# Two fused blocks with PEER experts on one core: more tokens by fetched rows, thirty expert blocks in float32, part of the gates on ScalarE

## The reference

```python
def peer_ffn(h, w_query, sub_keys_1, sub_keys_2, expert_u, expert_v):
    ...
    best, pos = lax.top_k(cand, PEER_TOPK)                 # 16 of the candidates, for each of 8 heads
    idx = jnp.take_along_axis(cand_idx, pos, axis=-1)      # expert numbers
    g = jax.nn.softmax(best, axis=-1)
    u = expert_u[idx]
    act = jax.nn.gelu(jnp.einsum('td,thkd->thk', xc, u))
    w = g * act
    return jnp.einsum('thk,thkd->td', w, expert_v[idx])
```

## Time and profile before

| | |
|---|---|
| runs | 1281.8, 1286.84, 1285.42 us; median 1285.42 |
| profiled execution | 1281.33 us, its span 1280.0 us |
| TensorE busy | 1222.2 us, 95% of the span, 11350 matmuls |
| VectorE busy | 1037.5 us, 81% |
| ScalarE busy | 641.9 us, 50% |
| GpSimd busy | 308.0 us, 24% |
| mean granted clock of TensorE | 0.994 |
| moved by DMA | 266.41 MB, mean 208 GB/s |

### The profile page before, as it was taken

The page is one execution under the profiler, slowest core; times in us unless marked ns, Lnnn a source line. Parts: engine busy times, 40 slices in busy tenths (PEclk is TensorE's granted clock), DMA queues, the critical chain, the costliest instruction groups (busy, mean ns, idle before and its releaser), DMA issues.

```text
span 1280.0 us, 26647 instructions
## 1 busy us (share of the span) xinstructions
PE 1222.2 (95%) x11350; PEld 1033.1 (81%) x11350; DVE 1037.5 (81%) x1640; ACT 641.9 (50%) x859; POOL 308.0 (24%) x202
## 2 busy tenths in 40 slices
PE   6899888999999999999999999999999999999997
PEld 5545674888844546648998899999999999999996
DVE  5865884899956776777499999999998888989884
ACT  5663231767635435646245455554445554445553
POOL 0322221154500000000102600000003656555640
PEclk9999998999999999999999999999999999999999
DMA  7530003755566322357165675555558999999981
GB/s 308 189 118 12 2 2 132 284 210 197 204 225 250 108 101 97 134 196 251 47 235 199 238 263 204 198 198 198 198 191 302 343 344 359 364 340 388 342 318 34
DMA packets 51350, 266.41 MB, mean 208 GB/s; under 512 B 5136, under 2 KB 5408, under 8 KB 32544
## 3 DMA queue, kind: packets, MB, share of 16 engines
q1 hardware_dynamic: 40192, 226.76, 49.3%
q0 software_dynamic: 10160, 35.96, 7.4%
q10 hardware_dynamic: 880, 1.99, 0.5%
HBM read 262.04 MB, written 2.10 MB: 206 GB/s over the span
## 4 chain that ended last, share of the span: by engine, by line
PE 65%; DVE 21%; DMA 5%; issue 4%; ACT 4%; ACTq 0%; POOL 0%; DVEq 0%; POOLq 0%
PE bank L674 18%; PE bank L677 18%; PE bank L680 18%; DMA arena<-in_expert_rows,arena 5%; PE bank L1103 2%; DVE X L2263 2%; DVE HT L2263 2%; DVE ring L2263 2%; PE bank L1317 2%; DVE arena L2316 1%; PE bank L754 1%; PE bank L1281 1%; DVE ring L1780 1%; PE bank L821 1%; PE bank L1270 1%
## 5 line engine op out<-in xcount | busy, mean ns | idle before, releaser
L674 PE MATMUL bank<-arena 128*128 128x256 f16 (+3 forms) x720 | 216.3, 307 | 0.6 <-DVE arena L1450 0.4
L677 PE MATMUL bank<-arena 128*128 128x256 f16 (+3 forms) x720 | 216.2, 307 | 0.0
L680 PE MATMUL bank<-arena 128*128 128x256 f16 (+3 forms) x720 | 216.1, 307 | 0.0
L1450 DVE SCALAR_TENSOR_TENSOR arena<-ring,arena 128x2048 f16<-128x2048 f32 (+1 forms) x59 | 133.8, 2273 | 31.8 <-ACT arena L2492 31.7
L3186 POOL DMA_INDIRECT arena<-in_expert_rows,arena x32 | 74.2, 2318 | 285.0 <-DVE arena L2316 283.9
L2492 ACT ACTIVATE arena<-ring 128x2048 f16<-128x2048 f32 (+1 forms) x59 | 111.2, 1891 | 28.9 <-PE bank L680 28.9
L2929 ACT CAST arena<-arena 128x448 f16<-128x448 f32 x64 | 36.0, 565 | 136.1 <-PE bank L680 133.7
L3186 POOL DMA_INDIRECT arena<-in_expert_v,arena x32 | 85.9, 2685 | 62.9 <-DVE arena L2334 54.2
L2263 DVE SCALAR_TENSOR_TENSOR HT<-ring,HT 128x2048 f16<-128x2048 f32 x41 | 93.8, 2287 | 8.0 <-ACT HT L2898 7.9
L680 PEld LDWEIGHTS bank<-arena 128*128 128x128 f16 x720 | 70.5, 98 | 36.8 <-issue 0.6
L674 PEld LDWEIGHTS bank<-arena 128*128 128x128 f16 x720 | 70.5, 98 | 36.7 <-issue 2.0
(11 more groups left out here) (382 smaller groups left out, 3713.2 us busy)
## 6 DMA issues: line engine op xcount, KB each, us to landing
ring<-in_expert_u SPq DMA_DIRECT2D x64, 1024.0 KB
ring<-in_expert_v SPq DMA_DIRECT2D x64, 1024.0 KB
ring<-in_w_in_n SPq DMA_DIRECT2D x24, 1024.0 KB, 4.7
ring<-in_w_up_t SPq DMA_DIRECT2D x22, 1024.0 KB, 5.0
ring<-in_w_down_n SPq DMA_DIRECT2D x11, 1024.0 KB, 4.8
ring<-in_w_out_n SPq DMA_DIRECT2D x8, 1024.0 KB, 4.7
ring<-in_w_query_t SPq DMA_DIRECT2D x8, 1024.0 KB, 4.8
ring<-in_w_in_t SPq DMA_DIRECT2D x3, 1024.0 KB
```

Of the source, the lines that this page charges most:

```text
L674: pe.matmul(out_, stat[0], mov[0], start=start, stop=False, skip_group_check=shared)
L677: pe.matmul(out_, stat[0], mov[1], start=False, stop=False, skip_group_check=shared)
L680: return pe.matmul(out_, stat[1], mov[0], start=False, stop=stop, skip_group_check=shared)
L1450: nv.scalar_tensor_tensor(out=lo, in0=ld.slot(i), scalar=W_UP, in1=hi, op0=ALU.mult, op1=ALU.subtract).then_inc(s["split_lo"], 1)
```

## The change

NG becomes 56 tokens, in three groups of 32, 16 and 8 tokens: in a fetch of the second group a token has 8 partitions, in one of the third 16. There are 56 fetches from each matrix, so 112, into NFETCH = 4 buffers, of which one is free early and the others when the search has ended. NT becomes 200 and there are 25 groups of gates. 48 of the 56 row dots are moved into turns 28 to 63 of the u stage. Whole blocks are now 30: 0, 1, 2, every third up to 63, and 28, 34, 40, 46, 52, 58. Split blocks in u use two pairs of buffers; the third lies where float32 tokens are kept, which whole blocks need to the end. `rows_gained` moves the multiplication of `h_rows` by the gain from GpSimd to VectorE. The last one-hot operation moves from VectorE to ScalarE, `gated_hi`, eight activations per group, each with a scale per partition. The small DMAs that place rows grow from 4 to 28, those for places and gates from 8 to 56.

```diff
-NG = 32
+ROW_GROUPS = (32, 16, 8)
+NG = sum(ROW_GROUPS)
+NFETCH = 4
 NT = S - NG
-WHOLE = 3
+WHOLE = [q for q in range(64) if q < 3 or q % 3 == 0 or (q > 26 and q % 6 == 4)]
+SPLIT = [q for q in range(64) if q not in WHOLE]
...
-ROWS_IN = [max(0, min(NG, 5 * (n - 63) // 4)) for n in range(128)]
-ROWS_OUT = [max(0, min(NG, n - 90)) for n in range(128)]
-ROW_GELU = 90
+ROWS_IN = [max(0, min(NG, 4 * (n - 27) // 3 if n < 64 else n - 15)) for n in range(128)]
+ROWS_OUT = [max(0, min(NG, (15 * (n - 72)) // 14)) for n in range(128)]
+ROW_GELU = next(n for n in range(128) if ROWS_IN[n] == NG) + 1
...
             for hf in range(2):
-                pe.matmul(ps.tile("fin", 1, hf)[128 - NG:128, :], m.row_sel, m.row_sums[:, hf * 512:(hf + 1) * 512],
-                          start=True, stop=True)
+                for a, sel in enumerate(m.row_sel):
+                    pe.matmul(ps.tile("fin", 1, hf)[:, :], sel, m.row_sums[a][:, hf * 512:(hf + 1) * 512],
+                              start=(a == 0), stop=(a == len(m.row_sel) - 1))
...
-        c = step(nv.tensor_tensor(oh2[:, 1], oh2[:, 0], of[3], ALU.mult))
-        after(c)
-        nv.tensor_tensor(oh2[:, 0], oh2[:, 0], of[2], ALU.mult).then_inc(s["one_hots"], 1)
+        nv.tensor_tensor(oh2[:, 1], oh2[:, 0], of[3], ALU.mult).then_inc(s["one_hots_lo"], 1)
...
+    def rows_gained():
+        nv.wait_ge(s["rows_placed"], 16 * sum(128 // n for n in ROW_GROUPS))
+        nv.wait_ge(s["row_gain_landed"], 16)
+        for h_ in m.h_rows:
+            nv.tensor_tensor(h_, h_, m.row_gain, ALU.mult).then_inc(s["h_rows"], 1)
...
-        expert_lo(q + 2 - WHOLE)
+        if q >= 62 or q + 2 in SPLIT:
+            expert_lo(SPLIT.index(q + 2) if q < 62 else len(SPLIT) + q - 62)
...
+    def gated_hi(g):
+
+        t0, oh2 = NG + 8 * g, m.oh2[g % 2]
+        na.wait_ge(s["one_hots_lo"], g + 1)
+        for i in range(8):
+            one = oh2[:, 0, i // 2, :, i % 2]
+            ins = na.activation(one, one, ACT.Copy, scale=m.slot_scale[:, t0 + i:t0 + i + 1])
+        ins.then_inc(s["one_hots"], 1)
...
-        expert_hi(q + 3 - WHOLE)
+        if q >= 61 or q + 3 in SPLIT:
+            expert_hi(SPLIT.index(q + 3) if q < 61 else len(SPLIT) + q - 61)
+        if q + 2 in GATES_IN:
+            gated_hi(GATES_IN[q + 2])
         if q in GATES_IN:
             keep_gates(GATES_IN[q])
...
+    for n, first in zip(ROW_GROUPS, ROW_FIRST):
+        of, to = slice(first, first + n), slice(first, first + n)
+        for i in range(128 // n):
+            rows, at = slice(i * n, (i + 1) * n), slice(i * n, (i + 1) * n)
+            ng.dma_start(m.row_at[rows, to], m.places[of, at]).then_inc(s["rows_placed"], 16)
+            ng.dma_start(m.row_gate[rows, to], gate[of, at]).then_inc(s["rows_placed"], 16)
...
-    read += [ps.full("u", q) if q < WHOLE else (s["expert_lo"], q - WHOLE + 1) for q in range(64)]
+    read += [ps.full("u", q) if q in WHOLE else (s["expert_lo"], SPLIT.index(q) + 1) for q in range(64)]
```

More of the change, by code:

```diff
@@ L30 @@
 NSLOTS = 5
-NG = 32
+ROW_GROUPS = (32, 16, 8)
+NG = sum(ROW_GROUPS)
+ROW_FIRST = [sum(ROW_GROUPS[:a]) for a in range(len(ROW_GROUPS))]
+NFETCH = 4
 NT = S - NG
-NK = 128 // NG
 GROUPS = NT // 8
-WHOLE = 3
+WHOLE = [q for q in range(64) if q < 3 or q % 3 == 0 or (q > 26 and q % 6 == 4)]
+SPLIT = [q for q in range(64) if q not in WHOLE]
 LATE = 26
@@ L424, in memory @@
     m.halves_h, m.halves_l = ([f16(b_[:, 1024 * i:1024 * (i + 1)]) for b_ in (x_, spare, ht)] for i in range(2))
+    m.row_gate, m.row_dots = (a.take(NG) for _ in range(2))
+    m.row_sel = [late[0][:, 128 * i:128 * (i + 1)] for i in range(len(ROW_GROUPS))]
+    m.slot_scale = m.rows[:, 0:256]
     a = Arena(t, 32768, END)
@@ L428, in memory @@
     g = Arena(t, 128 * NT, 32768)
-    m.h_rows = g.take(1024)
+    later = [g.take(1024) for _ in range(NFETCH - 4 + len(ROW_GROUPS))]
+    assert 32768 - 4 * 1024 >= g.at
+    g = Arena(t, 32768 - 4 * 1024, 32768)
+    m.h_rows = [g.take(1024) for _ in ROW_GROUPS]
     m.row_sums = m.h_rows
-    m.fetched = [g.take(1024) for _ in range(3)]
+    m.fetched = [g.take(1024) for _ in range(4 - len(ROW_GROUPS))] + later
+    m.early_fetches = 4 - len(ROW_GROUPS)
+    m.row_gain = m.fetched[m.early_fetches - 1]
     g = Arena(t, 33792, END)
     m.row_at = g.take(NG).bitcast(U32)
-    m.row_gate, m.row_dots, m.row_sel = (g.take(NG) for _ in range(3))
-    a = Arena(t, 16384, 128 * NT)
+    a = Arena(t, 16384, 32768 - 4 * 1024)
     m.qq = a.take(16, 256)
@@ L1277, in expert_in_whole @@
         b = ps.take(pe, "u", q)
+        between = gates(GATES_IN[q]) if q in GATES_IN else iter(())
         pe.wait_ge(*ld.landed(ld.u[q]))
@@ L2887, in expert_hi @@
     def expert_hi(n):
-        i, kk = k.expert(n), n % 3
+        i, kk = k.expert(n)
         na.wait_ge(*ld.landed(i))
@@ L2891, in expert_hi @@
             na.wait_ge(s["x_kept"], 32)
[L2892 to L2897, removed]
+        if n >= len(SPLIT) + 3:
+            na.wait_ge(s["v_done"], n - len(SPLIT) - 2)
+        else:
+            before = [q for q in SPLIT[:n] if (q - 1) % 3 == kk] if kk < 2 else WHOLE
+            if before:
+                na.wait_ge(*ps.full("u", before[-1]))
         na.activation(m.halves_h[kk], ld.slot(i), ACT.Copy, scale=W_UP).then_inc(s["expert_hi"], 1)
@@ L2918, in keep_gates @@
         if g == 0:
-            na.wait_ge(s["rows_placed"], 16 * 3 * NK)
+            na.wait_ge(s["rows_placed"], 16 * 3 * sum(128 // n for n in ROW_GROUPS))
         for hf in range(2):
@@ L3168, in gpsimd_program @@
     choose(0)
     ng.wait_ge(s["slots_named"], 1)
[L3170 to L3174, removed]
-    choose(1)
-    ng.wait_ge(s["rows_placed"], 16 * 3 * NK)
-    ng.wait_ge(s["row_gain_landed"], 16)
@@ L3186, in gpsimd_program @@
+    choose(1)
+    ng.wait_ge(s["rows_placed"], 16 * 3 * sum(128 // n for n in ROW_GROUPS))
+    for n in range(2 * NG):
+        if n == m.early_fetches - 1:
+            ng.wait_ge(s["h_rows"], len(ROW_GROUPS))
+        if n == m.early_fetches:
+            ng.wait_ge(*ps.free("slots", 1))
+        if n >= NFETCH:
+            ng.wait_ge(s["rows_used"], n - NFETCH + 1)
         ng.indirect_dma_start(
-            out=m.fetched[n % 3], out_offset=None, in_=k.d["expert_rows" if n < NG else "expert_v"],
+            out=m.fetched[n % NFETCH], out_offset=None, in_=k.d["expert_rows" if n < NG else "expert_v"],
```

89 lines of the change are left out of this document (51 added, 38 removed).

## The result

The changed kernel takes 1323.9 us (median of 4, 1320.2 to 1327.0) against 1283.6 us (median of 4, 1281.2 to 1286.8): ratio 1.032, 95% interval 1.030 to 1.034. It is slower by 40 us. I had forecast no change, 1284, and a range up to 1304.

The account below looks back on a forecast made before the run. TensorE, busy 95% of the span, was taken to bound the kernel, with DMA taking over in v by a little. From 1281.3 us, u adds 25.6 and v saves 23.0, giving 1283.9, about 1284 us; range 1258 to 1304.

Parts of the forecast that it names:

- the new wait: u from block 28: ScalarE waits for the load behind a whole block, so TensorE waits for gated one-hots; 30.3 us.
- late-u term: Waits in u from block 28: three cycles of 4.2 us, two of 6.8 and a last 4.1, 30.3 us.
- my 360.0: Whole u stage: 325.9 of TensorE work plus waits of 0.5, 3.3 and 30.3 us, against 334.4 before.
- my sum: Profiled execution: 1281.3 + 25.6 for u - 23.0 for v = 1283.9 us.
- 30.3 + 3.3: TensorE's waits in late u: 30.3 us from block 28 on, and 3.3 us at block 26.
- upper bound of 40: Waits in u from block 28: 40 us if fetches slow each landing by 1.5 us.
- 122.5: u blocks 0 to 25: 11 whole and 15 split blocks, 0.7 transposes, 0.5 waits; 122.5 us, not 132.6.
- They can't be issued earlier: u from block 28: the late waits would be nothing if loads were there in time, which was ruled out.
- DMA thus takes over from TensorE as bound: v stage: DMA's 271 to 272 us bounds it by a little, over TensorE's 263.7.
- my 272: v stage: 98.0 MB at 375 GB/s, 261 us, plus 10 us after the last landing and the start's slack.
- The fast rival: u costs only +10 us and v, bound by TensorE, takes 272.2; 1262 us in all; chance 0.27.
- The slow rival: v stage: DMA saturates at 347 GB/s, v takes 298.9 us, 1304 us in all; chance 0.18.

Follow-up runs that it names:

- experiment 4: Changed kernel without 48 of the 56 fetches of first-product rows and their row dots in u (output not the reference's): 1303.5 us, ratio 1.016.
- experiment 6: experiment 1 with the loads of split blocks issued ahead of the next whole block's load on SP's queue: 1293.0 us, ratio 1.009.
- experiment 1: Changed kernel with blocks 28, 34, 40, 46, 52 and 58 split again instead of whole: 1303.7 us, ratio 1.016.
- experiment 8: experiment 6 with the gain multiplication after the first one-hots and the reloads near block 40 of v spread out: 1285.6 us, ratio 1.002.
- experiment 9: experiment 8 with gates in block 26 and otherwise only slots 0 and 1, and the load order from block 27 on only: 1260.3 us, ratio 0.983.
- experiments 2 and 5: Changed kernel with, in 2, gates ahead of the high half in ScalarE's turn, 1340.6 us; in 5, gates in blocks q % 6 = 2 to 5, 1327.8 us.
- experiment 10: experiment 9 with the fourth one-hot operation back on VectorE: 1269.0 us, ratio 0.990.

## Why the prediction was wrong

**Right.** The prices per block (4.12, 5.41), the 27.5 us of placing DMAs, the row_sel matmuls (5.8 us for 5.5), and the place and the mechanism of the new wait: the blocks named, 30, 36, 42, 49 and 55, are the long ones, and ScalarE waits for u loads at turns 28, 34, 40, 46, 52 and 58. v (279.3 for 278.5) is right by luck, as told below.

**The step that failed** is the size of the late-u term, "3 x 4.2 + 2 x 6.8 + 4.1 = 30.3 us", with a term put at nothing beside it, the half clock behind each wait. u came out 37.5 us over my 360.0, nearly all of the 38.7 by which the profiled execution (1322.6) exceeds my sum. Late u without any wait is 12 x 6.96 + 7 x 5.42 + 13 x 5.05 + 6 x 4.12 = 211.8 us by the measured prices, 203.8 by mine; it took 271.7. The difference splits so:
- TensorE idle 271.7 - 229.6 = 42.1 us, where I had 30.3 + 3.3: +8.5. Of it 1.8 are block 26's (5.1 for 3.3); the waits of blocks 30, 36 and 42 are 3.9, 6.8 and 5.1 for my 4.2 each, and that of 61 is 6.0 for 4.1. The late loads come after 6.8 us on average and not 5.7, 8.4 at block 34 (experiment 4: the fetches are 1.6 of the average), and the eight multiplications take 2.3 us and not 1.5, 0.29 each. The Trainium skill, "ScalarE: Activation LUTs", section What ACT_TABLE_LOAD costs, gives an operation with its scale from a tile 0.09 us more than one with a constant scale. By an estimate that is 0.28 with the 0.19 of the earlier trace rows: the trace agrees. I had an upper bound of 40 for the term, if each landing took 1.5 us more; it took 1.1 more;
- the rest of late u, which I put at nothing: 271.7 - 211.8 - 42.1 = 17.8 us. It is mainly matmuls at half clock. The records show the granted clock at 0.50 for 44.4 us of u, in seven stretches of 3.4 to 10.2 us; five began in a wait and two (blocks 26 and 30) up to 1.5 us after one had ended. TensorE stood idle for 12.6 of the 44.4 us and worked for 31.8. At the measured ratio (0.88 us for 0.45) half of that is lost, an estimate of 15.9 us; the other 1.9 I can't divide. This is the largest single part. The rows that I worked from show a clock of 1.00, and none of them holds a wait like the one that I forecast. But the trace of before has such idle time, 4.81 us, ahead of the expert stages, with the half clock behind it (timeline of PE, then windows with columns as above):

```profile
197.64 1.94 PE L754 MATMUL bank<-cst,HT 128*128 128x128 f32 x8 [4.81 <-issue]
```

```profile
196.00:198.00 2.00, 0.36 (x2) 0.39 (x3) 1.93 (x5) 0.00 (x0) 0.00 (x0) 0.71 0.00 0
198.00:200.00 2.00, 2.00 (x9) 1.68 (x8) 1.90 (x5) 0.97 (x2) 0.85 (x1) 0.50 0.00 0
```

There the clock stays at 0.50 for 6.8 us (196.8 to 203.7), so the term could have been priced before the run. The Trainium skill, "TensorE: Matmul & The Clock Gate", Part 1, says that an idle TensorE falls to half its clock; the rows of block 36 agree, and I had left that rule out of the sum;
- gates in a whole block: 12 x 0.63 and some hundredths a block, 211.8 - 203.8 = 8.0. I priced them by the earlier trace rows, a split block;
- blocks 0 to 25: 125.8 for 122.5, +3.3 (block 3 takes 7.9 us, it waits 2.4 for the first low half).

8.5 + 17.8 + 8.0 + 3.3 = 37.6. The clock's part comes of the trace's arithmetic: no kernel kept the waits and not the half clock, so no run separates them. In the table above long gate waits and half clock go together.

**The other steps.** "They can't be issued earlier" may hold for the loads that it spoke of, those behind the six whole blocks 28 to 58: no run kept these blocks and changed the order. What I didn't see is that behind whole blocks at multiples of three the queue also holds back loads whose slots are free; experiment 6 freed blocks 28 to 43 of experiment 1's kernel by order alone. "DMA thus takes over from TensorE as bound" in v was wrong, and the right sum was luck: my 272 was DMA's steady limit, but experiment 8 shows TensorE's own time plus 2 us, 272.6. Of the other 6.7 us of the changed kernel 4.9 are the crowd at blocks 39 to 41 of v, and 1.7 lie at blocks 3 and 5. The fast rival's price of v, 272.2 and TensorE as the bound, is what experiments 8 and 9 reach; the changed kernel doesn't. The slow rival, DMA saturated at 347 GB/s, didn't come: the stage's mean is 358. The Trainium skill, "DMA: Bandwidth & Descriptors", section Specifications, has that same 358 GB/s as a core's limit; the mean of 365 in experiment 8 and 408 in the 2 us window above are over it, so for this core here it is no limit. The Trainium skill, "TensorE: Matmul & The Clock Gate", section Back-to-back issue gap, from which I had estimated 90 ns a matmul at 200 columns, stands above the 85.8 ns that were measured (4.12 us by 48).

**Open.** How much of the 40 us is the half clock's alone is an estimate, not a run. Which part of experiment 4's 20 us is fetches and which row dots isn't known. From block 63 to the first block of v it still takes 8.7 us in experiment 9 instead of 5.4.

## What to carry

When a block of work holds its buffer for longer than before, look at what stands behind its load in the queue: issue the loads whose buffers are free first, and put the late one where its reader is late as well. In these kernels a wait in a chain of in-order engines was not absorbed, and moving the waiting piece to another place in the cycle moved the cost or raised it (experiments 2 and 5). Where a forecast holds a long wait of TensorE, it needs a term for the half clock behind it: here some 16 us on 42.1 of idle.

## What the runs showed of the hardware

- A gate matmul of 128 float16 columns costs 0.058 us among float16 matmuls (0.93 by 16) and 0.096 among float32 ones (1.54 by 16).
- ScalarE's Copy of 128 float16 elements scaled per partition comes every 0.29 us (2.34 by 8) where the trace of before had 0.19 for 144 elements of a bank.
- A load of 1 MB took 5.2 us on average (4.6 to 6.0) from the end of its slot's last reader to ScalarE's start without fetches beside it, and 6.8 (5.5 to 8.4) with them, though the DMA share over late u is 0.68.
- The granted clock fell from 1.00 to 0.50 within a TensorE wait of 6.84 us and stayed there for 10.2 us, over six of them with matmuls back to back. It fell to 0.50 as well 1.2 us after the end of a TensorE wait of 2.55 us (experiment 10, block 57), while experiment 9 has a wait of 3.1 us at the end of u and a clock of 1.00 all through u.
